# A PEER expert stage with units of 128 tokens, and with units of 4 slots of 32 tokens

## What is computed

```
q = (xc @ wq).reshape(c, PEER_HEADS, 2, PEER_HALF)
s1 = jnp.einsum('chd,kd->chk', q[:, :, 0], k1)
s2 = jnp.einsum('chd,kd->chk', q[:, :, 1], k2)
v1, i1 = lax.top_k(s1, PEER_TOPK)
v2, i2 = lax.top_k(s2, PEER_TOPK)
cand = (v1[..., :, None] + v2[..., None, :]).reshape(c, PEER_HEADS, PEER_TOPK * PEER_TOPK)
sc, ci = lax.top_k(cand, PEER_TOPK)
expert = ia * PEER_KEYS + ib
gate = jax.nn.softmax(sc, axis=-1)
a = jnp.einsum('chkd,cd->chk', u_tab[expert], xc)
wgt = gate * jax.nn.gelu(a)
return jnp.einsum('chk,chkd->cd', wgt, v_tab[expert])
```

## Time and profile before

| what | value |
|---|---|
| median of three runs | 1936.55 us (1925.83 to 1940.11) |
| span of the profiled execution | 1932.6 us |
| PE busy, instructions | 1477.8 us (76%), 4385 |
| DVE busy | 1073.3 us (56%) |
| POOL busy | 1271.4 us (66%) |
| ACT busy | 372.7 us (19%) |
| mean granted clock of TensorE | 0.937 of full speed |
| gathers: 1088 issues by POOL | 571.18 MB, 77.3% of 16 DMA engines' span |
| first U gather issued | 380.92 us after the span's start |

### The profile page before, as it was taken

How to read it: one execution, slowest core, us unless ns; L and a number is a source line. 1 busy time by engine, 2 the same in 40 slices (tenths; PEclk the granted TensorE clock), 3 DMA queues, 4 the chain that set the end, 5 groups by cost and what they waited for, 6 DMA issues and landing times.

```text
span 1932.6 us, 14654 instructions
## 1 busy us (share of the span) xinstructions
PE 1477.8 (76%) x4385; PEld 627.3 (32%) x4385; DVE 1073.3 (56%) x2669; ACT 372.7 (19%) x891; POOL 1271.4 (66%) x1303
## 2 busy tenths in 40 slices
PE   7096478697959977777997776789867777777789
PEld 3055256242314422222442222234322222222233
DVE  4932441486785884445499444447964444444430
ACT  1023223102212211111221111112211111111111
POOL 2902820067777677777777777777777777777773
PEclk9598668899989989999998999999999999999999
DMA  7004407179999899999999999999999999999996
GB/s 304 16 24 89 139 26 319 39 247 321 342 351 381 301 346 402 410 408 409 410 336 346 361 374 372 404 410 362 347 353 374 388 410 408 409 409 409 409 402 231
DMA packets 171053, 618.32 MB, mean 320 GB/s; under 512 B 19728, under 2 KB 25184, under 8 KB 169984
## 3 DMA queue, kind: packets, MB, share of 16 engines
q0 software_dynamic: 156928, 571.18, 77.3%
q1 hardware_dynamic: 14048, 46.22, 7.0%
...
## 4 chain that ended last, share of the span: by engine, by line
PE 24%; DMA 19%; POOL 16%; DVE 15%; issue 7%; ACT 1%; DVEq 0%; ACTq 0%
PE sb_peer_acc L1540 19%; DMA sb_kept_V<-peer_v,sb_kept_expert 17%; POOL sb_peer_U L1180 9%; POOL sb_kept_V L1189 7%; DVE sb_peer_U L1346 4%; PE sb_peer_pq L1465 4%; DMA sb_peer_U<-peer_u,sb_kept_expert 1%; DVE sb_peer_hot L1281 1%; DVE sb_peer_f L1284 1%; DVE sb_peer_idx L1233 1%; DVE sb_peer_idx L1225 1%; DVE sb_peer_left L1226 1%; DVE sb_peer_val L1230 1%; DMA sb_peer_U<-peer_u,sb_peer_es 1%; DVE sb_peer_hot L1283 1%
## 5 line engine op out<-in xcount | busy, mean ns | idle before, releaser
L1540 PE MATMUL sb_peer_acc<-sb_kept_V,sb_peer_dg 128*128 128x512 f32 (+1 forms) x2176 | 1051.9, 619 | 311.7 <-DMA sb_kept_V<-peer_v,sb_kept_expert 205.1
L1346 DVE CUSTOM_DVE_ANT_0 sb_peer_U<-sb_peer_U,sb_rows_xn 128x1024 f32<-128x1024 f32 x512 | 619.6, 1223 | 546.4 <-DMA sb_peer_U<-peer_u,sb_kept_expert 536.7
L1540 PEld LDWEIGHTS sb_peer_acc<-sb_kept_V,sb_peer_dg 128*128 128x128 f32 (+1 forms) x2176 | 380.9, 189 | 958.5 <-issue 504.2
L1189 POOL DMA_INDIRECT sb_kept_V<-peer_v,sb_kept_expert x512 | 550.2, 1075 | 168.8 <-issue 93.5
L1180 POOL DMA_INDIRECT sb_peer_U<-peer_u,sb_kept_expert x512 | 522.2, 1020 | 185.0 <-issue 151.1
L1422 ACT ACTIVATE sb_peer_dg<-sb_kept_ident,sb_peer_wt 128x128 f32<-128x128 f32 (+1 forms) x544 | 210.6, 395 | 1069.8 <-PE sb_peer_acc L1540 841.4
L1180 POOL DMA_INDIRECT sb_peer_U<-peer_u,sb_peer_es x32 | 43.0, 1344 | 142.5 <-DVE sb_peer_es L1285 122.2
L1465 PE MATMUL sb_peer_pq<-sb_rows_wq,sb_peer_xnT 128*128 128x512 f32 x256 | 114.2, 599 | 1.1 <-ACT sb_peer_xnT L1374 1.1
L459 PE MATMUL sb_proj_pz<-sb_proj_w_in,sb_proj_xT 128*128 128x512 f32 (+1 forms) x192 | 73.4, 544 | 8.1 <-DVE sb_proj_xT L317 8.1
L1465 PEld LDWEIGHTS sb_peer_pq<-sb_rows_wq,sb_peer_xnT 128*128 128x128 f32 x256 | 49.0, 192 | 63.8 <-issue 62.3
L459 PEld LDWEIGHTS sb_proj_pz<-sb_proj_w_in,sb_proj_xT 128*128 128x128 f32 x192 | 37.9, 200 | 42.7 <-issue 41.1
...
...
## 6 DMA issues: line engine op xcount, KB each, us to landing
sb_peer_U<-peer_u,sb_kept_expert POOLq DMA_INDIRECT x512, 6.6
sb_kept_V<-peer_v,sb_kept_expert POOLq DMA_INDIRECT x512, 6.6
...
```

Source lines behind the costliest of these rows:

```text
L1189: pool.indirect_dma_start(V[:, m % RV, :], None, d["peer_v"], bass.IndirectOffsetOnAxis(ap=rows(m), axis=0)).then_inc(s_v[m % RV], 16)
L1346: dve.tensor_tensor_reduce(U[:, n % RU, :], U[:, n % RU, :], x, 1.0, 0.0, ALU.mult, ALU.add, a[:, g % 2, n % GRP:n % GRP + 1]).then_inc(s_ ...
L1540: mm = pe.matmul(acc[:r, c, :], dg[:, n % RD, 0:r], V[:, n % RV, c * 512:(c + 1) * 512], start=(s == 0), stop=(s == count[k] - 1))
```

## The change

The prompt tiles are now worked like the sample rows. A **part** is 32 tokens (p = 0 for the sample rows, then four per prompt tile, 17 in all), and a part has 32 units. In a unit, quadrant q holds the 32 tokens of the part at a slot of heads 2q and 2q+1. So the count of units, of gathers and of bytes gathered stays, and so do the shapes of dots and routes.

- The token rows of a part are copied to the four quadrants by SP (`spread`, two buffers of `xs`), ahead of a store.
- `dg` has 32 columns instead of 128. The product of a unit is four matmuls of 32x256: quadrant q of `acc` takes columns 256q to 256q+255. `acc` has two banks, used by parts in turn.
- The query of a part takes all 8 heads for 32 tokens: 32 matmuls of 32x512 in place of 8 of 128x512.
- There is one route per part instead of four per tile, 32 units apart, and `best`, `sums` and `numbers` stand 4 units apart with dots between them. `gates` stand 10 units after `numbers`.
- `result` adds four pieces of 32x256 per part, 38 units after the part.
- The turn of the next tile's rows stands 46 units into a tile, no longer at its start, and ACT's copy of it 48 units into it.

```diff
-        xs = S.sb("xs", [P, D])
+        xs = S.sb("xs", [P, 2, D])
...
+        parts = [(0, 0)] + [(k, b) for k in range(1, NT) for b in range(4)]
...
-        TURN_OUT = 2
-        ROWS_OUT, QTURN, QUERY_OUT, SCORE, EXPS, ROUTE, GATES = 3, 4, 7, 8, 22, 50, 62
-        query = {(1, b): 8 * (b - 1) for b in range(1, 4)}
-        query.update({(k, b): first[k - 1] + 6 + 8 * b for k in range(2, NT) for b in range(4)})
+        ROWS_OUT, QTURN, QUERY_OUT, SCORE, EXPS = 3, 4, 7, 8, 26
+        BEST, SUMS, NUMBERS, GATES = 50, 54, 58, 68
+        TURN, TURN_OUT = 46, 48
+        query = {(1, 1): 0}
+        query.update({(k, b): QS * (part(k, b) - 2) - 8 for k, b in parts[3:]})
-        RESULT = LAG + 2
+        RESULT = LAG + 4
...
+                def spread(p):
+                    k, b = parts[p]
+                    sp.wait_ge(s_xn, k + 1)
+                    if p >= 2:
+                        sp.wait_ge(s_dot, QS * (p - 1))
+                    for q in range(4):
+                        sp.dma_start(xs[quarter[q], p % 2, :], K.xn[quarter[b], order[k], :]).then_inc(s_xs[p % 2], 16)
...
+                for p in range(NP):
+                    spread(p)
+                    if p >= 3:
+                        store(p - 3)
...
-                    tt(K.x[:r, i, :], K.x[:r, i, :], acc[:r, :, :].rearrange("p a b -> p (a b)"), ALU.add).then_inc(s_y, 1)
+                    dve.wait_ge(s_mm, QS * (p + 1))
+                    for q in range(4):
+                        c = K.x[quarter[b], i, q * QN:(q + 1) * QN]
+                        ins = tt(c, c, acc[quarter[q], p % 2, 0:QN], ALU.add)
...
-                    for kb in due(n, ROUTE):
-                        route(*kb)
+                    for kb in due(n, BEST):
+                        best(*kb)
+                    for kb in due(n, SUMS):
+                        sums(*kb)
+                    for kb in due(n, NUMBERS):
+                        numbers(*kb)
...
-                    dst, src = (dg[:, n % RD, :], K.ident[:, :]) if k else (dg[:, n % RD, 0:NSMP], ident4[:, :])
-                    act.activation(dst, src, ACT.Copy, scale=wt[:, g % 2, n % GRP:n % GRP + 1]).then_inc(s_dg, 1)
+                    act.activation(dg[:, n % RD, :], ident4[:, :], ACT.Copy, scale=wt[:, g % 2, n % GRP:n % GRP + 1]).then_inc(s_dg, 1)
...
-                    for c in range(2):
-                        mm = pe.matmul(acc[:r, c, :], dg[:, n % RD, 0:r], V[:, n % RV, c * 512:(c + 1) * 512],
-                                       start=(s == 0), stop=(s == count[k] - 1))
+                    for q in range(4):
+                        mm = pe.matmul(acc[quarter[q], p % 2, 0:QN], dg[:, n % RD, :], V[:, n % RV, q * QN:(q + 1) * QN],
+                                       start=(n % QS == 0), stop=(n % QS == QS - 1))
```

124 lines of the change are left out of this document (58 added, 66 removed).

## The result

The changed kernel takes 1945.74 us (median of 11 runs, 1938.43 to 1950.32), the kernel before in the same series 1935.4 us (median of 11, 1925.83 to 1946.19). The ratio is 1.0063, with a 95% interval of 1.0039 to 1.0087: slower by 0.6%, where the prediction had it faster by 1.1%. The profiled execution of the changed kernel has a span of 1946.2 us, against 1932.6 before.

What follows compares the result with a forecast made beforehand. It took the gather pace, with POOL issues held by dots, as the bound. Tail -17, routing -5, copies +5 and waits +1 made -16, from 1932.6 to 1916 us; it said 1915, range 1868 to 1965.

Steps and rivals of the forecast that it cites:

- What bounds the kernel: Expert stage: gathers set the pace, POOL issues starting inside a dot are held; the middle's excess is 108.7 us.
- Tail, -17: After the last U issue: faster products on four column groups let V issues run at full gather rate, saving 17 us.
- Empty buffers, -29: Middle: POOL's waits for dots when U buffers are spent behind route blocks, about 29 us, would go.
- Routing, 6.9 us per part: Middle: the spread routes' loss in each of 15 parts, making the excess 103.5 instead of 108.7 us, -5.
- the catch-up of 3.8: Each part: pieces and result delay dots by 11.0 us, costing POOL 0.34 per us, 3.8 us.
- the slow pace behind it, 3.1: Each part: 0.23 us more per unit for two thirds of the 20 units between numbers and next best.
- the slow pace becomes the usual one: Rival for the middle: spread pieces leave no quiet stretch, 11.3 us per part, +45, 1978 us; chance 0.21.
- the forecast's own case (5 to 9.8): Middle losing 5 to 9.8 us per part, total time 1888 to 1956 us; chance 0.52.
- The sign that was set for it: U issue of unit 32 to that of unit 543: more than 1440 us means the slow pace has won.
- Copies, +5: Middle: SP's token-row copies of 0.52 MB per part take gather time, 20 us if all shows, taken as +5.
- Waits for gelu: ACT's turned_out ahead of a gelu, three times, delays a dot about 3.5 us each; +1 in all.
- Query block: Rival: 9.6 us of queries on PE makes DVE wait for a gelu each part, +10, 1926 us; no separate chance.

Runs made afterwards that it cites:

- e4: The changed kernel with each part's token rows copied by VectorE into PSUM, where the dots read them; 1874.68 us, ratio 0.9704 to the kernel before.
- e12: The changed kernel with the token rows copied by VectorE once per part into a second SBUF buffer, which the dots read; 1958.94 us, ratio 1.0152.
- e8: The changed kernel with routing from part 7 on replaced by tiny instructions, later parts reusing part 6's expert numbers; 1884.9 us in one run.
- e3: The kernel before with only the changed routing schedule, one route per 32 units in three pieces, without copies or column groups; 1963.7 us, ratio 1.0177.
- e2: The changed kernel with each route as one block at offset 50 instead of three pieces four units apart; 2006.49 us, ratio 1.0373.
- e1: The changed kernel without its token-row copies from part 2 on, dots reusing rows of parts 0 and 1; 1948.91 us, ratio 1.0057.

## Why the prediction was wrong

- **What bounds the kernel: right.** POOL issues are held by dots, and the middle is the place. e4 and e12 show why: the second SBUF operand.
- **Tail, -17: right**, measured -16.0. The last two V issues stand 1.28 us apart, as assumed, and the last product starts 8.8 us behind the last V issue. A unit's products took 1.08 us in most of the tail, 0.64 in the rest and at its end, not the 0.46 worked out of the earlier trace rows, which is a run of 64 without a pause. It cost nothing, since 1.08 is below 1.28. The busy table gives the clock granted in the two stretches, 0.61 on the mean and 1.00:

```profile
1888.00:1936.00 48.00, 32.28 (x264) 7.34 (x264) 6.30 (x14) 10.50 (x34) 34.38 (x37) 0.61 1.02 402
1938.00:1942.20 4.20, 2.25 (x32) 0.56 (x24) 0.04 (x1) 0.00 (x0) 0.00 (x0) 1.00 0.28 110
```

- **Empty buffers, -29: right.** POOL's waits for dots after unit 32 are gone.
- **Routing, 6.9 us per part: wrong**, and this is the step that failed. Measured are 9.2 per part, and the middle moved by +28.8 where its sum had +1 (-5 for routing, +5 for copies, +1 for waits). Split at the fourth dot behind each route's numbers, the trace of the changed kernel loses 4.0 us per part in the pieces and their catch-up, and 4.6 in the 20 units up to the next best (means of the 14 routes that have a next one, with POOL's place interpolated between U issues). So the catch-up of 3.8 was sized about right. What was mis-sized is the slow pace behind it, 3.1 by "two thirds of the 20 units", read off the bursts of before: 4.6 is 0.23 for all 20. It is not one slow pace that lasts. Each part's start and result throw the dots out once more, which the sum had at less than 0.5 per part (5 us of copies over 15 parts and 0.4 us of a result's delay); e8, with no routes, loses 2.8 per part.
- **The rival that came nearest** is "the slow pace becomes the usual one". Its reason, that the same 15 disturbances spread out cost more, is what e3 shows; its 1978 was too high by 32 us. By its own price, from 9.9 us per part upward, the kernel is not there: 9.2 is the upper end of the forecast's own case (5 to 9.8). The sign that was set for it, more than 1440 us from U32 to U543, is there with 1443, by less than executions of this kernel differ (1938 to 1950).
- **What weighed against it was read wrongly**: that the bursts of before held overload which spreading would take away. It did take it away (29 us), but e2 and the rows of before show that a bunch pays it only once in four, and e3 that spreading loses more than that; the two busy tables place the loss in the quiet stages, which went.
- **Copies, +5: at most that.** e1 shows none at this pace, which is what the working said of a slow stage. **Waits for gelu:** there, three of 4.1 to 4.2 us where 3.5 was the estimate, as DVE's line shows. **Query block:** too small to be seen in any run.

```profile
DVE sb_peer_U L1374 <- ACT sb_peer_ga L1447: 12.3, 3, 4.2
```
